# Second FFN of a hybrid diffusion layer on one Trainium2 core: its up products by a Strassen scheme of seven block products, tokens in two halves

## The reference

```python
def rmsnorm(x, w):
    return x * lax.rsqrt(jnp.mean(x * x, axis=-1, keepdims=True) + NORM_EPS) * w

def swiglu(h, w13, w2):                      # w13: 1024 x 2*2816, w2: 2816 x 1024
    a, b = jnp.split(h @ w13, 2, axis=-1)
    return (jax.nn.silu(a) * b) @ w2

h = rmsnorm(x, norm_w[2]) * (1.0 + m[7]) + m[6]
x = x + 0.5 * m[8] * swiglu(h, ffn2_w13, ffn2_w2)
y = rmsnorm(x, final_norm)
```

## Time and profile before

| | us |
|---|---|
| median of 3 runs | 2940.4 (2939.18 to 2944.02) |
| span of the profiled execution (first to last instruction) | 2931.8 |
| PE busy | 2805.0, 96% of the span |
| DVE / ACT / POOL busy | 1535.5 / 803.7 / 455.9 |
| mean granted TensorE clock | 0.984 of full |

### The profile page before, as it was taken

The page is one execution under the profiler, slowest core; times in us unless marked ns, Lnnn a source line. Parts: engine busy times, 40 slices in busy tenths (PEclk is TensorE's granted clock), DMA queues, the critical chain, the costliest instruction groups (busy, mean ns, idle before and its releaser), DMA issues. The chain is left out here.

```text
span 2931.8 us, 53464 instructions
## 1 busy us (share of the span) xinstructions
PE 2805.0 (96%) x21936; PEld 2672.4 (91%) x21936; DVE 1535.5 (52%) x2793; ACT 803.7 (27%) x1410; POOL 455.9 (16%) x545
## 2 busy tenths in 40 slices
PE   7999999999999999999799987999999999999998
PEld 3999999999998989999688865899899999999997
DVE  4456566556636346533587857455633333333335
ACT  4211111111114233454266644222511111111111
POOL 4100110111003101222243423123300000000001
PEclk8999999999999999999899989999999999999999
DMA  6112222222102334334654441321111111111111
GB/s 274 58 61 84 86 79 78 79 86 86 59 28 96 123 126 152 125 139 178 193 123 113 87 152 71 123 92 42 58 44 43 41 36 38 42 41 39 35 37 71
DMA packets 187486, 257.67 MB, mean 88 GB/s; under 512 B 99104, under 2 KB 137376, under 8 KB 185664
## 3 DMA queue, kind: packets, MB, share of 16 engines
q1 hardware_dynamic: 172480, 227.79, 23.6%
q0 software_dynamic: 12608, 27.48, 2.9%
q10 hardware_dynamic: 2240, 0.13, 0.1%
HBM read 200.23 MB, written 55.12 MB: 87 GB/s over the span
## 5 line engine op out<-in xcount | busy, mean ns | idle before, releaser
L873 DVE SCALAR_TENSOR_TENSOR x<-bank,gate,x 128x128 f32<-128x128 f32 (+1 forms) x832 | 409.7, 515 | 199.9 <-PE bank L1003 199.3
L1058 ACT ACTIVATE act_out_ffn<-bank 128x384 f32<-128x384 f32 x132 | 64.9, 491 | 1268.3 <-PE bank L974 1268.3
L1061 DVE TENSOR_TENSOR g_ffn<-act_out_ffn,bank 128x384 f32<-128x384 f32 x132 | 73.2, 554 | 617.7 <-ACT act_out_ffn L1058 617.7
L974 PE MATMUL bank<-h_hi_ffn,wlo_a_ffn 128*128 128x384 f32 x1056 | 358.5, 339 | 10.1 <-DVE h_lo_ffn L668 7.3
L974 PE MATMUL bank<-h_hi_ffn,whi_a_ffn 128*128 128x384 f32 x1056 | 356.2, 337 | 0.0
L974 PE MATMUL bank<-h_lo_ffn,whi_a_ffn 128*128 128x384 f32 x1056 | 356.2, 337 | 0.0
L974 PE MATMUL bank<-h_hi_ffn,wlo_b_ffn 128*128 128x384 f32 x1056 | 355.3, 336 | 0.0
L974 PE MATMUL bank<-h_lo_ffn,whi_b_ffn 128*128 128x384 f32 x1056 | 355.2, 336 | 0.0
L974 PE MATMUL bank<-h_hi_ffn,whi_b_ffn 128*128 128x384 f32 x1056 | 355.2, 336 | 0.0
L1003 PE MATMUL bank<-g_hi_ffn,wlo_d_ffn 128*128 128x384 f32 x1056 | 354.5, 336 | 0.0
L1003 PE MATMUL bank<-g_hi_ffn,whi_d_ffn 128*128 128x384 f32 x1056 | 353.2, 334 | 0.0
(11 more groups left out here) (302 smaller groups left out, 4903.6 us busy)
## 6 DMA issues: line engine op xcount, KB each, us to landing
ada_beside_ffn<-in_ada_w POOLq DMA_DIRECT2D x96, 256.0 KB, 3.5
raw_a_ffn<-in_ffn_w SPq DMA_DIRECT2D x44, 512.0 KB, 4.5
raw_b_ffn<-in_ffn_w SPq DMA_DIRECT2D x44, 512.0 KB, 5.1
raw_d_ffn<-in_ffn_w SPq DMA_DIRECT2D x44, 512.0 KB, 3.7
raw_in<-in_w_in SPq DMA_DIRECT2D x35, 512.0 KB, 5.1
mix<-row_out SPq DMA_DIRECT2D x23, 576.0 KB, 3.2
sc_ar<-streams SPq DMA_DIRECT2D x36, 256.0 KB, 3.9
gates<-mix SPq DMA_DIRECT2D x16, 576.0 KB, 5.1
```

Of the source, the lines that this page charges most:

```text
L873: ins = nc.vector.scalar_tensor_tensor(xs, kit.banks[4 + d % 4][:, a:b], kit.gate[:, gate, d, cond:cond + 1], xs, ALU.mult, ALU.add)
L974: mm = nc.tensor.matmul(kit.banks[2 * slot + j][:, 0:CH], w[q][:, par, cols], v[:, k, toks], start=(k == 0 and m == 0), stop=(k == ku - 1 ...
L1058: return self.nc.scalar.activation(out, a, ACT.Silu)
L1061: self.nc.vector.tensor_tensor(g32, act_out, b, ALU.mult).then_inc(g32_ready, 1)
```

## The change

`program` calls `folded_ffn` for the second FFN and `folded_final` for the last norm in place of `ffn` and `final_norm`. In the following, p is the half of the tokens (0 or 1), t a chunk of 288 in it (C4; four chunks in all), j one of seven block products.

- **Up products.** For a hidden tile, the weights are a 2 x 2 block matrix (a or b; lower or upper four of the eight k), the normed tokens of a half another (lower or upper k; chunk 0 or 1). Seven products replace eight: j names the left blocks A11, S2, A22, S3, S1, A12, S4 and the right blocks B11, T2, T4, T3, T1, B21, B22. One product is 4 x 3 = 12 matmuls of 288 columns. The four S are sums of weight blocks, made anew for each tile by POOL (`sums`, four instructions of 512 columns); the T are sums of token blocks, made once for a half. Five additions with a PSUM operand on DVE (`second_sum`, `third_sum`, `c21`, `c22`, `c12`) and a copy on ACT (`first_product`) make a and b of both chunks. Four banks serve the seven products. The first tile of each half (Tile with plain=True) is done with the eight plain products, 96 matmuls.
- **Order.** Behind each product stands one down block of the pair before (`folded`). Up weights are loaded twice, once for each half, and so are the down weights. Hi and lo parts of the left blocks are seven instructions of 512 columns a tile on ACT and on DVE, each with a single buffer that comes free when its product is done.
- **Between halves** (middle) the last downs of half 0 and the right blocks of half 1 come together; the statistics of chunks 2 and 3 are in the first and last pair of half 0.
- **Last norm.** It works with chunks of 288 and scales x in place; x is stored from there. Its reciprocal for chunk 0 stands on DVE ahead of the adds of the last eight down blocks.

```diff
+A11, S2, A22, S3, S1, A12, S4 = range(7)
+B11, T2, T4, T3, T1, B21, B22 = range(7)
...
+    block = {B11: full[:, 0, lower], B21: full[:, 0, upper], B22: full[:, 1, upper],
+             T1: full[:, 0, lower], T4: full[:, 0, upper], T3: full[:, 1, lower], T2: full[:, 1, upper]}
+    left_from = lambda u, j: raw_b[:, 0:D // 2] if u.plain and j == S1 else source[j]
+    left_count = lambda u, j: u.n(1, 1 if j in DIRECT else 0)
...
+        def load(u, f, after_plain=False):
+            hold(left_ready[A11], u.n(1, 1))
+            if not after_plain:
+                hold(sum_ready[S2], u.n(1, 0))
+                hold(sum_ready[S3], u.n(1, 0))
+            sp.dma_start(raw_lower[:], up_a[f, :, 0:D // 2]).then_inc(s["lower_loaded"], 16)
+            hold(left_ready[A22], u.n(1, 1))
+            if after_plain:
+                hold(left_ready[S1], u.n(1, 1))
+            else:
+                hold(left_ready[S3], u.n(1, 0))
+                hold(sum_ready[S1], u.n(1, 0))
+            sp.dma_start(raw_b[:], up_b[f]).then_inc(s["b_loaded"], 16)
+            hold(left_ready[A12], u.n(1, 1))
+            if not after_plain:
+                hold(sum_ready[S4], u.n(1, 0))
+            sp.dma_start(raw_upper[:], up_a[f, :, D // 2:D]).then_inc(s["upper_loaded"], 16)
+        def load_down(i, f):
+            hold(s["wd_ready"], i * 4)
+            for par in range(2):
+                sp.dma_start(raw_d[:, par], kit.dram[w2][f + par]).then_inc(s["d_loaded"], 16)
...
+    def t_sums(dve, p):
+        dve.wait_ge(right_ready[B11], p + 1)
+        nc.vector.tensor_tensor(full[:, 0, lower], full[:, 1, lower], full[:, 0, lower], ALU.subtract)\
+            .then_inc(s["t_summed"], 1)
+        dve.wait_ge(right_ready[B22], p + 1)
+        dve.wait_ge(s["t_summed"], p * 3 + 1)
+        dve.wait_ge(s["t3_summed"], p + 1)
+        nc.vector.tensor_tensor(full[:, 1, upper], full[:, 1, upper], full[:, 0, lower], ALU.subtract)\
+            .then_inc(s["t_summed"], 1)
+        dve.wait_ge(right_ready[B21], p + 1)
+        dve.wait_ge(s["t_summed"], p * 3 + 2)
+        nc.vector.tensor_tensor(full[:, 0, upper], full[:, 0, upper], full[:, 1, upper], ALU.subtract)\
+            .then_inc(s["t_summed"], 1)
+    def t3_sum(pool, p):
+        for half in range(2):
+            pool.wait_ge(full_ready[half], p * 8 + 8)
+        pool.wait_ge(s["t_summed"], p * 3 + 1)
+        pool.wait_ge(right_ready[T1], p * 2 + 1)
+        nc.gpsimd.tensor_tensor(full[:, 1, lower], full[:, 1, upper], full[:, 1, lower], ALU.subtract)\
+            .then_inc(s["t3_summed"], 1)
...
+        def first_product(t):
+            act.wait_ge(s["up_done"], t.n(7, 4, 1))
+            act.wait_ge(g32_ready[0], t.n(1, 1))
+            nc.scalar.activation(p1[:], bank[0], ACT.Copy).then_inc(s["p1_ready"], 1)
...
+        def even(t, u, before, sq=None):
+            silu_second(before)
+            down_high(t.i - 1, 1)
+            high(S4, t, before)
+            first_product(t)
+            g_high_second(t.i - 1)
+            high(A11, u, t)
+            if sq is not None:
+                for i in range(4):
+                    square(act, 0, sq, i)
+            high(S2, u, t)
+            high(A22, u, t)
+            high(S3, u, t)
+            high(S1, u, t)
+            silu_first(t)
+            high(A12, u, t)
+            if sq is not None:
...
+    def low(dve, j, u):
+        dve.wait_ge(left_hi_ready[j], left_count(u, j) + 1)
+        nc.vector.tensor_tensor(left_lo[:, j], left_from(u, j), left_hi[:, j].bitcast(F32), ALU.subtract)\
+            .then_inc(left_ready[j], 1)
...
+        def g_low_second(i):
+            for par in range(2):
+                dve.wait_ge(g_hi_ready[1], i * 2 + (par + 1))
+                nc.vector.tensor_tensor(g_lo[:, par, 1], u2[:, par], g_hi[:, par, 1].bitcast(F32), ALU.subtract)\
...
+        def second_sum(t):
+            dve.wait_ge(s["up_done"], t.n(7, 4, 2))
+            dve.wait_ge(s["p1_ready"], t.n(1, 0, 1))
+            need(dve, g_ready[1], t.i * 2)
+            nc.vector.tensor_tensor(u2[:, t.par], bank[1], p1[:], ALU.add).then_inc(s["u2_ready"], 1)
+        def third_sum(t):
+            dve.wait_ge(s["up_done"], t.n(7, 4, 4))
+            nc.vector.tensor_tensor(u3[:], bank[1], p1[:], ALU.add).then_inc(s["u3_ready"], 1)
+        def c21(t):
+            dve.wait_ge(s["u3_ready"], t.n(1, 0, 1))
+            nc.vector.tensor_tensor(p1[:], bank[3], u3[:], ALU.add).then_inc(s["c21_ready"], 1)
+        def c22(t):
+            dve.wait_ge(s["up_done"], t.n(7, 4, 5))
+            dve.wait_ge(s["c21_ready"], t.n(1, 0, 1))
+            nc.vector.tensor_tensor(u3[:], bank[2], u3[:], ALU.add).then_inc(s["c22_ready"], 1)
+        def c12(t):
+            dve.wait_ge(s["up_done"], t.n(7, 4, 7))
+            dve.wait_ge(s["u2_ready"], t.n(1, 0, 1))
+            nc.vector.tensor_tensor(u2[:, t.par], bank[2], u2[:, t.par], ALU.add).then_inc(s["c12_ready"], 1)
+        def even(t, u, before):
+            i, p = t.i - 1, t.p
+            g_second(before)
+            down_low(i, 1)
+            low(dve, S4, t)
+            add_to_x(i, 0, 0, p)
+            g_low_second(i)
+            low(dve, A11, u)
+            second_sum(t)
+            add_to_x(i, 0, 1, p)
+            low(dve, S2, u)
+            add_to_x(i, 0, 2, p)
+            low(dve, A22, u)
+            third_sum(t)
+            c21(t)
+            add_to_x(i, 0, 3, p)
+            low(dve, S3, u)
+            c22(t)
+            add_to_x(i, 0, 4, p)
+            low(dve, S1, u)
+            add_to_x(i, 0, 5, p)
+            g_first(t)
+            low(dve, A12, u)
+            c12(t)
+            add_to_x(i, 0, 6, p)
+            add_to_x(i, 0, 7, p)
...
+        def odd(t, u, before, down=True, made=None):
+            i, p = t.i - 1, t.p
+            add = (lambda d: add_to_x(i, 1, d, p)) if down else (lambda d: None)
+            if not before.plain:
+                g_second(before)
+            g_low(before)
+            low(dve, S4, t)
+            add(0)
+            if u is not None:
+                low(dve, A11, u)
+            second_sum(t)
+            add(1)
+            if u is not None and not u.plain:
+                low(dve, S2, u)
+            add(2)
+            if u is not None:
+                low(dve, A22, u)
+            third_sum(t)
+            c21(t)
+            add(3)
+            if u is not None and not u.plain:
+                low(dve, S3, u)
+            down_low(t.i, 0)
+            c22(t)
+            add(4)
+            if made is not None:
+                reciprocal(dve, made)
+            if u is not None:
+                low(dve, S1, u)
+            add(5)
+            g_first(t)
+            if u is not None:
+                low(dve, A12, u)
+            if made is not None:
+                normed(dve, made, 0)
+            g_low(t)
+            c12(t)
+            add(6)
+            add(7)
+            if made is not None:
...
+        block_low(dve, T1, 0)
+        block_low(dve, B22, 0)
+        t_sums(dve, 0)
+        low(dve, S2, t1)
+        sum_low(dve, T2, 0)
+        g_first(t0)
+        sum_low(dve, T4, 0)
+        low(dve, S3, t1)
+        sum_low(dve, T3, 0)
+        low(dve, A11, t1)
+        low(dve, A12, t1)
+        low(dve, A22, t1)
+        g_second(t0)
+        low(dve, S1, t1)
+        sum_low(dve, T1, 0)
+        odd(t1, Tile(1, 0, 0), t0, down=False)
+        pair(1, 0, 2)
+        with dve.Fori(2, pairs - 1) as i:
+            pair(i, 0)
...
+    def gpsimd(pool):
+        def sums(u):
+            a, b1, b2 = raw_lower[:], raw_b[:, 0:D // 2], raw_b[:, D // 2:D]
+            pool.wait_ge(s["b_loaded"], u.n(16, 16, 16))
+            need(pool, left_ready[S1], u.n(1, 1))
+            nc.gpsimd.tensor_tensor(tmp[S1][:], b1, b2, ALU.add).then_inc(sum_ready[S1], 1)
+            pool.wait_ge(s["lower_loaded"], u.n(16, 16, 16))
+            pool.wait_ge(sum_ready[S1], u.n(1, 0, 1))
+            nc.gpsimd.tensor_tensor(b1, a, b1, ALU.subtract).then_inc(sum_ready[S3], 1)
+            need(pool, left_ready[S2], u.n(1, 0))
+            nc.gpsimd.tensor_tensor(tmp[S2][:], tmp[S1][:], a, ALU.subtract).then_inc(sum_ready[S2], 1)
+            pool.wait_ge(s["upper_loaded"], u.n(16, 16, 16))
+            need(pool, left_ready[S4], u.n(1, 0))
+            pool.wait_ge(sum_ready[S2], u.n(1, 0, 1))
+            nc.gpsimd.tensor_tensor(tmp[S4][:], raw_upper[:], tmp[S2][:], ALU.subtract).then_inc(sum_ready[S4], 1)
...
+        def product(t, j, after_plain=False, fresh=False):
+            pe.wait_ge(left_ready[j], left_count(t, j) + 1)
+            if fresh:
+                pe.wait_ge(right_ready[j], rights(t.p, j) + (2 if j == T1 else 1))
+            if j == 0:
+                pe.wait_ge(s_ready[0], t.n(1, 1))
+            elif j == 1:
+                pe.wait_ge(*((g32_ready[1], t.n(1, 1)) if after_plain else (s["u3_ready"], t.n(1, 0))))
+            elif j == 2:
```

(63 more changed lines are left out.)

546 lines of the change are left out of this document (added).

## The result

| | us |
|---|---|
| changed kernel, median of 4 runs | 2972.4 (2969.95 to 2975.61) |
| kernel before, 4 runs beside it | 2942.2 (2939.18 to 2944.62) |
| ratio | 1.0106, 95% interval 1.0091 to 1.012 |
| predicted | 2935, range 2905 to 2968 |
| profiled execution: time / span | 2974.0 / 2972.2 |

A forecast was written before the change was run, and what follows sets the result against it. PE, busy 96%, was taken as the bound. Span 2062.4 + 44.1 + 686.4 + 7.7 + 8 + 22 + 50.8 + 44.5 = 2925.9 us, plus 8.6 to the median: 2934.5, called 2935; range 2905 to 2968.

The forecast's parts named there:

- I take 130.0: PE: a matmul of 288 columns costs 130.0 ns, so 5832 take 758.2 us, 65.5 less than before.
- Rival 4: PE: a matmul of 288 columns costs 133.3 ns, 19 us more in all, 2954; chance 0.06.
- I take 1.1: Loop: PE waits 1.1 us a pair because POOL's sums delay DVE; 22 us over twenty pairs.
- the table's term: Twenty pairs with two statistics: predicted 724.1 us, measured 747.5, so 23.4 more.
- The middle, 50.8: Between the halves: 276 matmuls at 35.9 us plus waits of 5.5, 4.7 and 4.7, together 50.8 us.
- its term of 8 us for two pairs: Two pairs holding statistics: scale-and-shift ahead of Silu on ACT and norm work on DVE lose 4 us in each.
- The start edge: Second FFN's start to the first folded pair: 180 matmuls at 23.4 us, waits and half clock, together 44.1 us.
- tail: From the last folded matmul through the last norm to the end: 44.5 us, against 45.7 before.
- The median lies 8.6 above the span; I carry that.: Whole kernel: 8.6 us added to the predicted span of 2925.9 to give the median, 2934.5.
- 5 (longer edges, 15): Edges: blocks wait for DMA or an ACT table, the three edges cost 15 us more, 2950; chance 0.06.
- rival 3: Loop: DVE becomes the bound, second_sum 3 us late in even tiles, 38 us more, 2973; chance 0.18.

The follow-up runs named there:

- price kernel: Standalone kernel, none of the model computed: twelve-matmul blocks at several widths, then beside DVE and POOL work; 288 columns took 131.7 ns a matmul, 512 took 226.8.
- the run with small sums: Changed kernel with POOL's four sums a tile made on 16 of 512 columns, except each half's first sums; output not the reference's: 2929.3 us, ratio 0.9962.
- p5: Changed kernel with DVE's order in the loops and the DVE and ACT order at the edges both changed, sums still on POOL: 2941.1 us, ratio 0.9984.
- p8: Changed kernel with loop and edge orders changed, weight sums and T3 moved to DVE, c22 placed earlier: 2927.7 us, ratio 0.9944 to the kernel before.
- p2: Changed kernel with only DVE's order in the loops changed, second_sum and g_lo placed earlier, POOL's sums kept: 2948.8 us, ratio 1.0021.
- second price kernel: Standalone matmul timing at other widths, 64 to 480 columns, nothing else at work: 111.4 ns a matmul at 192 and 224 columns, 131.7 at 288.

## Why the prediction was wrong

Its mechanisms are all in the trace; its sizes were low in three places, and these add up where it had treated them as rivals of each other.

1. **"I take 130.0".** The step of a matmul of 288 columns was put at 0.4514 ns a column because 384 and 512 columns both gave that. It is 131.7 alone, with and without DVE and POOL at work, and 132.3 in the loop: 2.3 x 5832 = 13.4 us more (12.2 of them in the pairs). The bound beside it, 133.3, was nearer; what adds the last 0.6 in the loop is not shown. Rival 4 was given 0.06, and 70% of its 19 us came true. The row for 512 columns was taken from another stage, and the price kernel gives 226.8 for it, not 231; so the two points that seemed to lie on one line through zero did not.
2. **"I take 1.1".** Pauses in the pairs. `second_sum` of the even tile was late as walked, once a pair. The g_lo of the odd tile, which the working had "0.75 late" only if three sums came ahead of g_first, was late in nearly every pair too (11.9 us, 19 times, beside 15.1, 20 times). The sums cost 1.7 us a pair, 35.2 in all, for 22 predicted: 13.2 more. The two pairs with a norm and the two statistics came to 13.7 for 15.7 (in the run with small sums, 712.3 - 20 x 34.93), 2.0 less. That gives 12.2 + 13.2 - 2.0 = 23.4, the table's term.
3. **The middle, 50.8.** It took 60.2. The working had 14.9 us of waits and no half clock. Beyond its 276 matmuls (36.5) and 5.4 of half clock, 18.3 are waits of PE:

```profile
2507.90 0.37 PE L1846 MATMUL bank<-g_hi_ffn,wd_lo_ffn 128*128 128x288 f32 x1 [4.10 <-DVE x L1530]
...
2513.64 0.44 PE L1846 MATMUL bank<-g_lo_ffn,wd_hi_ffn 128*128 128x288 f32 x1
2513.88 0.44 PE L1846 MATMUL bank<-g_hi_ffn,wd_hi_ffn 128*128 128x288 f32 x1
...
2532.83 0.61 PE L1846 MATMUL bank<-g_hi_ffn,wd_lo_ffn 128*128 128x288 f32 x1 [6.74 <-DVE x L1530]
...
2557.60 0.58 PE L1809 MATMUL bank<-right_hi_ffn,left_lo_ffn 128*128 128x288 f32 x1 [4.30 <-DVE u_ffn L1589]
```

The first of these was walked as the wait for the block lo parts; it is mostly something else. Ahead of Silu on ACT stand the scale-and-shift instructions of chunk 3, so `g_second`, the down lo parts and the first adds behind it on DVE are late:

```profile
2502.84 2.18 ACT L1227 ACTIVATE h_full_ffn<-h_full_ffn,mod,scale 128x288 f32<-128x288 f32 x4 [0.67 <-DVE h_full_ffn L1245]
2504.93 0.42 ACT L1357 ACTIVATE u_ffn<-u_ffn 128x288 f32<-128x288 f32 x1
```

```profile
2505.39 0.46 DVE L1550 TENSOR_TENSOR u_ffn<-u_ffn 128x288 f32<-128x288 f32 x1 [2.58 <-ACT u_ffn L1357]
2505.91 1.29 DVE L1567 TENSOR_TENSOR wd_lo_ffn<-raw_d_ffn,wd_hi_ffn 128x512 fp32r<-128x512 f32 x2
```

The prediction had named those scale-and-shift instructions, in its term of 8 us for two pairs, but had not followed them past the last pair's end. (In p5, where they stand behind Silu and the adds ahead of the block lo parts, 2.3 us of this wait are left.) The second wait, for the T sums ahead of the adds, was walked at 4.7 and is 6.74: POOL's sums stretch them, the two sums behind T3 to 2.3 us each, where the first, alone, has 1.35. The third is `c22`, and it too is POOL's: 4.30 us here and 0.70 with small sums. Behind each of these three pauses matmuls follow 0.24 us apart, at half clock; 50 of them in the middle cost 50 x 0.108 = 5.4 us that the sum did not have.
4. **The start edge** is right to 4.3 us of 44.1. Its three waits are 4.9, 9.3 and 5.4 us, where 5.1, 8.1 and 2.6 were walked; the last is `c22`, put down to the landing of raw_b, but with small sums it is 1.2, so most of it comes from POOL's sums. The **tail** is right to 0.7 of 44.5, so the last norm in place costs what was said.
5. **"The median lies 8.6 above the span; I carry that."** What lies around a span is 1.8 us (2974.0 - 2972.2). The other 6.8 were the distance of a short execution from its median, and they came back as the later start of the second FFN (8.4). Two errors that nearly cancel.

By size the rivals add (rival 4's share stands partly in the edges too, 1.2 us): 4 came with 13.4 of its 19 us, 5 (longer edges, 15) with 4.3 + 9.4 + 0.7 = 14.4, 3 with 13 of its 38. The time it gives for rival 3, 2973, was met for another reason: DVE is not the bound, since p8 runs at 89% without a pause. The 65 us saved on PE were real but for those 13; with the waits in the loop gone, p8 ends 11.4 us ahead of the kernel before in this stretch (855.4 against 866.8). Its start edge and middle still take 14.9 and 19.2 us more than their 180 and 276 matmuls at 132.3 ns: that is where much of PE's saving goes.

Open: why the price of a matmul is uneven in its columns, how much of p2's gain is place and how much milder stretching, and how much of the two edges could be had with another layout of the blocks, which wasn't tried.

## What to carry to other kernels

Unknown costs that don't exclude each other (a price, the edges, a wait) belong in one sum with a common spread, not in separate rivals with small chances: here three of them came together. Before an engine's free time is counted as room for helpers, find which port they share: a sum on POOL took 0.85 us from DVE in the loop and 0.97 in a row of meetings, more than the 0.73 that DVE needs for it, and at a place that the landing of raw_b chose. And an order written out by hand is worth reading for what stands ahead of the one instruction that PE waits for: moving five instructions gave 24 us, while moving work out of an edge gave nothing until the next pair had room for it.

## What the runs showed of the hardware

- The step from matmul to matmul (float32r, weights changed each time) is not proportional to the columns: 111.7 ns at 192 and at 224, 120.0 at 256, 131.7 at 288, 173.3 at 384, 206.7 at 448, 226.8 at 512.
- A POOL instruction with two SBUF inputs costs DVE's instructions of that kind 0.97 us for its 1.36, and is itself slowed from 1.36 to 1.70: the two go in turn, 1.70 us for one of each, where one behind the other would take 2.09; DVE instructions with a PSUM input pass beside it.
- DVE at 89 and 86% busy, all of it in an order tied to PE's, leaves PE without a pause in stretches of 200 and 250 us (p8).
- In the second price kernel the clock was at 0.50 from 107.5 to 281.6 us, in the stretches of 64 and 128 columns, with PE never idle (283 matmuls in 60.00 us, PE busy 60.00), while in the changed kernel's FFN half clock always followed a pause. At half clock 64 and 128 columns cost the same, 213.3 ns.
